# Third group of probability transposes moved ahead of the projection halves in a hybrid attention encoder

## The reference

```
def attend(q_blk):                                   # one block of 128 queries
    s = jnp.einsum('bqhcd,bkhcd->bhcqk', q_blk, k).astype(jnp.float32) * scale
    s = jnp.where(key_ok, s, NEG)
    p = jax.nn.softmax(s, axis=-1)
    a = p[:, :, 0] - lam * p[:, :, 1]
    return jnp.einsum('bhqk,bkhv->bqhv', a.astype(v.dtype), v)
```

## Time and profile before

| | |
|---|---|
| runs | 1888.45, 1895.43, 1899.31 us; median 1895.43 us |
| profiled execution | 1886.95 us |
| its span, first to last instruction | 1885.6 us |
| mean granted clock of the matrix engine | 0.965 |
| PE busy | 1707.6 us (91%) |
| weight loads (PEld) busy | 1584.6 us (84%) |
| DVE, ACT busy | 1100.9 us (58%), 886.8 us (47%) |
| dense passes of the first layer, of the second | about 572 to 858 us, 1491 to 1776 us of the span |

### The profile page before, as it was taken

How to read it: one execution, slowest core, us unless ns; L and a number is a source line. 1 busy time by engine, 2 the same in 40 slices (tenths; PEclk the granted TensorE clock), 3 DMA queues, 4 the chain that set the end, 5 groups by cost and what they waited for, 6 DMA issues and landing times.

```text
span 1885.6 us, 35772 instructions
## 1 busy us (share of the span) xinstructions
PE 1707.6 (91%) x13754; PEld 1584.6 (84%) x13754; DVE 1100.9 (58%) x2533; ACT 886.8 (47%) x2652; POOL 402.9 (21%) x390
## 2 busy tenths in 40 slices
PE   3799999999998999989989989999998898888896
PEld 2798899999887788768989989999998878776796
DVE  6585584345537777783185845834453575667616
ACT  4434545345506666682063344452553374647603
POOL 5430221220111002011373103113103001012044
PEclk9999999999989999899999999999998999899998
DMA  7200100200020111142121001012001111103312
GB/s 256 69 24 13 57 23 27 77 23 13 32 78 15 38 31 38 46 143 96 37 103 53 24 14 56 23 34 70 26 13 59 50 29 31 47 22 128 121 46 90
DMA packets 97705, 102.44 MB, mean 54 GB/s; under 512 B 7488, under 2 KB 87600, under 8 KB 97280
## 3 DMA queue, kind: packets, MB, share of 16 engines
q1 hardware_dynamic: 96576, 99.08, 16.3%
q10 hardware_dynamic: 960, 1.07, 0.2%
HBM read 70.43 MB, written 21.17 MB: 49 GB/s over the span
## 4 chain that ended last, share of the span: by engine, by line
PE 70%; DVE 16%; ACT 6%; POOL 3%; issue 2%; DMA 2%; SPq 0%; DVEq 0%; ACTq 0%
PE psum L856 45%; PE psum L996 7%; PE psum L931 3%; PE psum L1143 3%; PE psum L1050 3%; DVE row_max L1906 3%; PE psum L1127 2%; ACT p_b L1441 2%; DVE p_b L1920 2%; PE psum L1036 1%; POOL w_lo L822 1%; PE psum L903 1%; ACT aT_b L1451 1%; PE psum L979 1%; PE psum L974 1%
## 5 line engine op out<-in xcount | busy, mean ns | idle before, releaser
L856 PE MATMUL psum<-w_hi,hT_hi 128*128 128x256 f32 x1824 | 529.2, 290 | 6.2 <-POOL w_lo L822 4.3
L856 PE MATMUL psum<-w_hi,hT_lo 128*128 128x256 f32 x1824 | 516.6, 283 | 0.0
L856 PE MATMUL psum<-w_lo,hT_hi 128*128 128x256 f32 x1824 | 516.3, 283 | 0.0
L818 POOL CAST w_hi<-w_raw 128x512 fp32r<-128x512 f32 (+1 forms) x168 | 109.6, 652 | 1319.4 <-DMA w_raw<-in_w_in 791.5
L856 PEld LDWEIGHTS psum<-w_hi,hT_hi 128*128 128x128 f32 x1824 | 347.6, 191 | 14.8 <-POOL w_lo L822 5.1
L856 PEld LDWEIGHTS psum<-w_hi,hT_lo 128*128 128x128 f32 x1824 | 347.5, 191 | 0.0
L856 PEld LDWEIGHTS psum<-w_lo,hT_hi 128*128 128x128 f32 x1824 | 347.4, 190 | 0.0
L856 PE MATMUL psum<-hT_hi,w_hi 128*128 128x346 f32 (+1 forms) x672 | 229.8, 342 | 24.6 <-DVE hT_lo L1565 9.3
L856 PE MATMUL psum<-hT_hi,w_lo 128*128 128x346 f32 (+1 forms) x672 | 220.9, 329 | 0.0
L856 PE MATMUL psum<-hT_lo,w_hi 128*128 128x346 f32 (+1 forms) x672 | 220.6, 328 | 0.0
L822 POOL TENSOR_TENSOR w_lo<-w_raw,w_hi 128x512 fp32r<-128x512 f32 (+1 forms) x168 | 211.4, 1258 | 25.9 <-DVE neg_max L1907 14.1
(11 more groups left out here) (161 smaller groups left out, 2618.6 us busy)
## 6 DMA issues: line engine op xcount, KB each, us to landing
w_raw<-in_w_in SPq DMA_DIRECT2D x72, 256.0 KB, 3.5
w_raw<-in_w_in SPq DMA_DIRECT2D x28, 512.0 KB, 4.2
h_dram<-hbuf SPq DMA_DIRECT2D x16, 512.0 KB, 2.6
w_raw<-in_w_out SPq DMA_DIRECT2D x16, 512.0 KB, 4.1
hbuf<-h_dram SPq DMA_DIRECT2D x16, 512.0 KB, 5.9
qk_b<-y_dram SPq DMA_DIRECT2D x16, 512.0 KB, 3.2
y_dram<-y_stage SPq DMA_DIRECT2D x96, 64.0 KB, 1.6
qk_t<-rot SPq DMA_DIRECT2D x56, 86.5 KB, 2.1
```

The source lines that it names most:

```text
L818: pool.tensor_copy(hi, raw).then_inc(w_hi_done, 1)
L856: last = nc.tensor.matmul(out_ap, lhs[a](k), rhs[b](k), start=k == 0 and a + b == 0, stop=k == KT - 1 and b == 1)
```

## The change

The third group of transposes is issued directly behind the first two, and the first two projection halves of the step follow in one run. Nothing is added or taken away, the banks and the numbers of the semaphores stay as they are, and the other engines' programs are the same.

```diff
                 pe.wait_ge(b_comb, B_STEP[l, g, t])
                 transposes(t, 0)
                 transposes(t, 1)
+                transposes(t, 2)
                 for x, half in parts[:1]:
                     project(l, nx, "qk", x, half)
-                transposes(t, 2)
                 for x, half in parts[1:2]:
                     project(l, nx, "qk", x, half)
                 values(t, range(6))
```

## The result

The changed kernel takes 1902.43 us (median of 8 runs, 1895.08 to 1907.53), the kernel before 1893.16 us in the runs beside it (8 runs, 1888.45 to 1899.31). The ratio is 1.0047, with a 95% interval of 1.0024 to 1.0069: slower by some 9 us (4.5 to 13 us by the interval). A ratio of 1 lies outside the interval, so the change does cost time; whether it costs more or less than half a per cent stays open.

The account below looks back on a forecast made before the run. Steps with two or three halves were taken as bound by the matrix engine alone. 11.6 - 0.9 + 0.75 = +11.4 us, +0.61%, gave 1907 us on the median of 1895.43 us, range 1897 to 1914 us.

Parts of the forecast that it names:

- two-half steps: Dense-pass steps with two projection halves: bound by the matrix engine alone at 8.55 us, anything added paid in full.
- The new wait: Ahead of the third group, PE waits 0.48 us for ACT's copy from bank 0; the first half's later start costs 0.50 us.
- the merge: Joining two projection runs into one loses a short load interval after transposes, costing 0.05 us a step.
- the term of the 21 steps: Steps with two or three halves and no long wait of their own: 0.55 us each, 11.6 us together.
- Steps with a long wait: Six steps in second-layer B1 and B2, already waiting elsewhere, costed apart: together -0.9 us.
- tiles 1 and 4 of B1 and B2: Second layer: existing waits, 1.01 us for a bank and 2.84 us for `combine`, absorb the delay; cost nothing.
- tile 2: Second-layer B1 and B2: third group lies inside the wait for DVE's rotary step, saving 0.32 and some 0.6 us.
- One-half steps: Six 7.12 us steps set by `combine`: PE becomes the later one, +0.07 us; 0.75 us in all, bounds 0 and 3 us.
- the first two terms: Of the forecast sum: 11.6 us for steps with two or three halves, 0.75 us for steps with one half.
- The clock didn't stay up: Rival, second-layer B1 and B2 long waits: shorter idle time keeps the clock up, about +8 us in total; chance 0.12.
- It didn't fall more often: Rival: second gaps in the 21 steps cost one 1.2 us low-clock stretch in each of six passes, +18.6 us; chance 0.05.
- the chain through ACT decides: Rival: an earlier third copy on ACT shortens steps with projections, -4.6 us in total; chance 0.03.

Follow-up runs that it names:

- second_group_first: Against the changed kernel: in the 33 steps with a projection the second group of transposes stands ahead of the first; ratio 1.0109 to the kernel before.
- long_waits_only: Against the kernel before: the change made only in tile 2 of passes B1 and B2 of the second layer; ratio 1.0000.
- best: Against the kernel before: six products of the first half ahead of the third group, except second-layer B1 and B2 tile 2, where the group leads; ratio 0.9997.
- third_last: Against the changed kernel: third group of transposes moved behind both projection halves, ahead of the values; ratio 1.0062 to the kernel before.

## Why the prediction was right

**The number.** The forecast was 1907 us in a range of 1897 to 1914; measured are 1902.43 us. Of the 5 us between them, 2.3 us are the median of the kernel before, which was 1893.16 us in the runs beside it and 1895.43 us in the three that the forecast started from. The rest is that the change was sized at 11.4 us and costs some 9. That matters for the chances: 0.70 were on a loss of more than half a per cent, and the measured 0.47% lies just on the other side, which had 0.27.

**What bounds.** As forecast: two-half steps are PE's alone. The change's 0.46 us and second_group_first's 0.78 us pass through in full.

**The new wait.** It is 0.48 us in each of these steps, as the steps without a projection had shown, and three products are enough to hide it. This was the right row to price the wait from.

**Its size in the step.** The forecast had 0.55 us; it is 0.46 us. The start of the third group (1.11 us) and the length of the unbroken run hold. What was mis-sized is the third group itself, which was taken at 0.37 us as "only moved". Behind a wait it takes less: the projection follows at 672.97, 0.28 us after 672.69. The rows showed it beforehand: the three loads take 0.31 us behind the wait in the earlier trace rows and 0.41 us in the stream in the earlier trace rows. So the third group starts at 1.11 us and takes 0.28 us, where the first half had started at 0.61 us and the third group had taken 0.37 us, and 0.05 us come from the merge: 1.11 + 0.28 - 0.61 - 0.37 + 0.05 = 0.46 us. With this the term of the 21 steps is 9.7 us and not 11.6.

**Steps with a long wait.** In tiles 1 and 4 of B1 and B2 nothing is lost: 11.46 us (11.48 before), 11.93 (11.93), 11.04 and 11.04 (11.04 and 11.05). Where the next transposes wait for `combine` in tile 4, they wait 2.38 and 2.37 us instead of 2.84 and 2.87. In tile 2 the changed kernel has 13.99 and 15.33 us, 0.2 and 0.6 us less, for 0.3 and 0.6 forecast. That they agree is in part luck: by what long_waits_only and best show, the clock moves these steps by more than that. That the group lies inside the wait is shown by the shorter idle time.

**One-half steps.** The change of bound came as worked out, but the price was 0.1 to 0.2 us and not 0.75. PE's way is 7.10 us where 7.19 was worked out, again by the third group's 0.28 us, so a step that had 7.12 us loses nothing. Only the step behind the last such pair is 0.18 us longer.

**The sum.** 9.7 + 0.1 - 0.8 = 9.0 us, against 9.3 us between the medians, whose interval is 4.5 to 13 us; it agrees no more closely than that, and the -0.8 us is the least certain term. The forecast of 11.4 us was too high by the first two terms, 1.9 and some 0.6 us.

**The rivals.** The clock didn't stay up: behind the shortened idle times of 3.48 and 3.94 us it is 0.50 (1.2 GHz) again. It didn't fall more often by the new gaps: in the six steps of B1 it is 1.00 (2.4 GHz), with 0.48 us of waiting in each, and in all dense passes together the trace has 11 stretches at 0.50, 56 us in all, and that of before 12, 58 us in all; second_group_first, with 0.81 us of waiting a step, has 10. The Trainium skill, "TensorE: Matmul & The Clock Gate", section "A second HAM failure mode: psum-queue depth-cycling", tells of a kernel in which short idle times of the engine between groups made it swing, and gives no size for them. At gaps of 0.48 us, 5% of the step besides the 0.36 us, this trace shows none of it. That the chain through ACT decides is what third_last shows, but only with the third group 1.9 us later; with the change ACT's third copy comes 0.2 us earlier and nobody waits for it.

## What to carry to other kernels

Work that stands between two groups which share a PSUM bank may be there as cover for the copy out of that bank. Before moving it, look for a step of the same kernel without such work: its wait is nearly the price (0.48 us there, 0.46 us here), and it is paid in every step that the engine bounds. Only as much cover is needed as the wait is long (here three products of twelve), and too much delay is paid as well, once what the chain through the next engines has in hand (here some 1.5 us) is used up.

## What was not expected of the hardware

Three transposes take 0.37 to 0.38 us from their first load to the next group's when products of 346 columns run ahead of them, and 0.28 us behind a wait of 0.48 us: in the stream their second load comes 0.16 us after the first, behind the wait 0.06 us. So 0.09 us of the wait are given back by what follows it; no run here shows why. The profiled executions differ by up to 7 us ahead of the first changed instruction, with granted clocks of 0.96 and 0.97 there; the difference of two profiled spans, 20 us, is more than twice what the change costs.
